# Seven-product MLP chunks: which engine makes which sum and low part, and in which order the loads come

## The reference, cut to what matters

```python
u = modulate(h, sh_f, sc_f)
y = jnp.square(jax.nn.relu(u @ mlp_w_up[layer])) @ mlp_w_down[layer]
h = layer_norm(DEEPNORM_ALPHA * h + (1 + g_f) * y, ...)
```

## Time and profile before

| | |
|---|---|
| median of 3 runs | 2198.15 us (2197.61 to 2199.14) |
| the profiled execution | 2198.61 us |
| its span, first to last instruction | 2196.9 us |
| TensorE's granted clock, mean | 0.997 of full speed |
| TensorE busy | 2144.9 us, 98% |
| VectorE, ScalarE, GpSimd busy | 1419.3, 820.0, 373.6 us |

### The profile page before, as it was taken

The page is one execution under the profiler, slowest core; times in us unless marked ns, Lnnn a source line. Parts: engine busy times, 40 slices in busy tenths (PEclk is TensorE's granted clock), DMA queues, the critical chain, the costliest instruction groups (busy, mean ns, idle before and its releaser), DMA issues.

```text
span 2196.9 us, 28310 instructions
## 1 busy us (share of the span) xinstructions
PE 2144.9 (98%) x9984; PEld 1730.2 (79%) x9984; DVE 1419.3 (65%) x2223; ACT 820.0 (37%) x1457; POOL 373.6 (17%) x273
## 2 busy tenths in 40 slices
PE   6999999999999999999999999999999999999998
PEld 5888888878887787788887876677888888888886
DVE  7423656578576676776768566767747547557556
ACT  4201445161224234233347456546222422422432
POOL 0000220010033032130200022321003303303304
PEclk9999999999999999999999999999999999999999
DMA  7434653314413423314122110211211021021021
GB/s 291 142 98 133 117 131 101 105 39 134 130 63 95 125 66 115 113 59 134 48 96 85 43 39 20 78 58 33 64 58 58 21 74 57 20 75 57 19 77 77
DMA packets 52433, 183.96 MB, mean 84 GB/s; under 512 B 7472, under 2 KB 7648, under 8 KB 52352
## 3 DMA queue, kind: packets, MB, share of 16 engines
q1 hardware_dynamic: 44640, 161.50, 22.8%
q0 software_dynamic: 4944, 16.96, 3.6%
q10 hardware_dynamic: 2768, 4.41, 0.5%
HBM read 174.43 MB, written 8.42 MB: 83 GB/s over the span
## 4 chain that ended last, share of the span: by engine, by line
issue 44%; PE 41%; POOL 8%; DVE 3%; ACT 2%; DMA 1%; SPq 1%; POOLq 0%; ACTq 0%; DVEq 0%
PE ps L2054 11%; PE ps L2056 11%; PE ps L2055 11%; POOL whi L678 4%; POOL wlo L678 2%; PE ps L2519 1%; POOL h_blocks L673 1%; PE ps L2549 1%; PE ps L2533 1%; DMA resid<-in_xt 1%; PE ps L2157 1%; PE ps L2298 1%; PE ps L2283 1%; PE ps L2287 1%; DVE stats L1572 0%
## 5 line engine op out<-in xcount | busy, mean ns | idle before, releaser
L2054 PE MATMUL ps<-uhi,whi 128*128 128x512 f32 x1152 | 451.6, 392 | 11.3 <-DVE wlo L1700 5.0
L2055 PE MATMUL ps<-ulo,whi 128*128 128x512 f32 x1152 | 448.4, 389 | 0.0
L2056 PE MATMUL ps<-uhi,wlo 128*128 128x512 f32 x1152 | 448.3, 389 | 0.0
L2054 PE MATMUL ps<-whi,uhi 128*128 128x512 f32 x704 | 288.2, 409 | 2.4 <-ACT resid L1111 2.2
L2056 PE MATMUL ps<-whi,ulo 128*128 128x512 f32 x704 | 276.1, 392 | 0.0
L2055 PE MATMUL ps<-wlo,uhi 128*128 128x512 f32 x704 | 275.4, 391 | 0.0
L2054 PEld LDWEIGHTS ps<-uhi,whi 128*128 128x128 f32 x1152 | 216.2, 188 | 65.2 <-issue 7.3
L1740 DVE TENSOR_TENSOR resid<-ps,resid 128x512 f32<-128x512 f32 x336 | 217.9, 680 | 54.8 <-PE ps L2056 53.7
L2056 PEld LDWEIGHTS ps<-uhi,wlo 128*128 128x128 f32 x1152 | 216.3, 188 | 45.3
L2055 PEld LDWEIGHTS ps<-ulo,whi 128*128 128x128 f32 x1152 | 216.3, 188 | 44.0
L1021 ACT ACTIVATE h_blocks<-ps 128x512 f32<-128x512 f32 x96 | 57.2, 596 | 516.5 <-PE ps L2056 516.5
(11 more groups left out here) (300 smaller groups left out, 3542.1 us busy)
## 6 DMA issues: line engine op xcount, KB each, us to landing
stage<-in_stream SPq DMA_DIRECT2D x276, 512.0 KB, 3.6
aux<-in_early SPq DMA_DIRECT2D x8, 512.0 KB, 7.1
early_place<-in_early SPq DMA_DIRECT2D x8, 512.0 KB, 14.2
resid<-in_xt SPq DMA_DIRECT2D x8, 512.0 KB, 15.9
resid<-in_x POOLq DMA_DIRECT2D x8, 512.0 KB, 9.5
resid_dram<-resid ACTq DMA_DIRECT2D x8, 512.0 KB, 2.6
resid<-resid_dram POOLq DMA_DIRECT2D x8, 512.0 KB, 3.6
out<-resid SPq DMA_DIRECT2D x7, 512.0 KB, 2.6
```

What stands on the lines that cost most here:

```text
L2054: pe.matmul(dst, left_hi, right_hi, start=start, stop=False, skip_group_check=more)
L2055: pe.matmul(dst, left_hi, right_lo, start=False, stop=False, skip_group_check=more)
L2056: return pe.matmul(dst, left_lo, right_hi, start=False, stop=stop, skip_group_check=more)
```

## The change

Four parts, all in the twelve chunks made of seven products; chunks 0 and 7 and the rest of the kernel stay as they are. The arithmetic is the same, the engines and the order differ.

- S2 (h7) and S4 (h8) are both made by VectorE in halves of 128x512 (`second_sum`, `fourth_sum`) among the half sums; GpSimd's S2 and its semaphore go.
- The low part of P2's weights (w_part 4, 2; B21) goes from GpSimd to VectorE, behind the low of h1.
- GpSimd's four other weight low parts each wait until VectorE has made the activation's low part of the same product (a new wait on `h_low` ahead of each). VectorE's order of adds and low parts changes; `up_low(8)` and `up_low(9)` move behind adds of P6.
- In the streamed chunks up-weight 2 comes after vector 1 and up-weight 3 after vector 2, so each stands one place earlier in the stream, and vector 3 comes among the last five.

```diff
@@ load_order @@
-            ada(SC_KV + c, range(3))
+            ada(SC_KV + c, range(2))
             w(W_MLP0 + 8 * c + 2)
-            ada(SC_KV + c, range(3, 4))
+            ada(SC_KV + c, range(2, 3))
             w(W_MLP0 + 8 * c + 3)
-            ada(SC_KV + c, range(4, K))
+            ada(SC_KV + c, range(3, K))
...
@@ GpSimd, seven_sums @@
-                pool.wait_ge(h_low, 8 * q0 + 3 + 8 * i)
-                pool.tensor_tensor(h_block(7), h_block(6), h_block(0), ALU.subtract).then_inc(h_sums_by_pool, 1)
-                def low_by_pool(n, hi, lo):
+                def low_by_pool(after, n, hi, lo):
+                    pool.wait_ge(h_low, 8 * q0 + after + 8 * i)
                     pool.wait_ge(operand_hi, 15 * q0 + n + 15 * i)
...
-                low_by_pool(7, 4, 2)
-                low_by_pool(9, 5, 0)
-                low_by_pool(11, 1, 7)
-                low_by_pool(13, 8, 6)
-                low_by_pool(15, 4, 3)
+                low_by_pool(5, 9, 5, 0)
+                low_by_pool(6, 11, 1, 7)
+                low_by_pool(7, 13, 8, 6)
+                low_by_pool(8, 15, 4, 3)
@@ VectorE, seven_chunk @@
+                def weight_low(hi, lo, n):
+                    v.wait_ge(operand_hi, 15 * q0 + n + 15 * i)
+                    v.tensor_tensor(w_part(lo), w_block(lo), fr(w_part(hi)), ALU.subtract).then_inc(w_low, 1)
...
+                def second_sum(f):
+                    v.wait_ge(h_sums, 7 * q0 + 2 + 3 * f + 7 * i)
+                    v.tensor_tensor(h_block(7)[:, f, :], h_block(6)[:, f, :], h_block(0)[:, f, :],
+                                    ALU.subtract).then_inc(h_sums, 1)
+                def fourth_sum(f):
+                    v.wait_ge(h_sums, 7 * q0 + 3 + 3 * f + 7 * i)
+                    v.tensor_tensor(h_block(8)[:, f, :], h_block(1)[:, f, :], h_block(7)[:, f, :],
+                                    ALU.subtract).then_inc(h_sums, 1)
...
                 if with_ada:
-                    for k in range(3):
+                    for k in range(2):
                         vector(k)
                 up_low(2)
                 if with_ada:
-                    vector(3)
+                    vector(2)
                 up_low(3)
...
-                    for k in range(4, K):
+                    for k in range(3, K):
                         vector(k)
                 half_sum(0)
                 half_low(0)
+                second_sum(0)
+                fourth_sum(0)
                 half_sum(1)
+                second_sum(1)
                 half_low(1)
-                add("P7", 0, 1, 2)
-                v.wait_ge(h_sums_by_pool, q0 + 1 + i)
-                v.tensor_tensor(h_block(8), h_block(1), h_block(7), ALU.subtract).then_inc(h_sums, 1)
-                add("P7", 3)
-                v.wait_ge(h_sums, 4 * q0 + 4 + 4 * i)
-                add("P4", 0)
+                fourth_sum(1)
+                add("P7", 0, 1, 2, 3)
+                v.wait_ge(h_sums, 7 * q0 + 7 + 7 * i)
                 low_of(4, 1, 6)
-                add("P4", 1, 2, 3)
+                weight_low(4, 2, 7)
+                add("P4", 0, 1)
                 low_of(5, 0, 8)
+                add("P4", 2, 3)
                 add("P2", 0, 1)
                 low_of(2, 7, 10)
                 add("P2", 2, 3)
                 add("P1", 0)
                 low_of(3, 6, 12)
-                add("P1", 1)
+                add("P1", 1, 2, 3)
+                low_of(4, 8, 14)
+                add("P6", 0, 1, 2)
                 up_low(8)
-                add("P1", 2, 3)
+                add("P6", 3)
                 up_low(9)
-                add("P6", 0)
-                low_of(4, 8, 14)
-                add("P6", 1, 2, 3)
                 add("P5", 0, 1, 2, 3)
```

More of the change, by code:

```diff
@@ L445, in build @@
         h_sums = sem("h_sums")
-        h_sums_by_pool = sem("h_sums_by_pool")
         h_low = sem("h_low")
@@ L1030, in seven_up @@
                         high(w_part(1), w_block(8))
-                        act.wait_ge(h_sums, 4 * q0 + 1 + 4 * i)
+                        act.wait_ge(h_sums, 7 * q0 + 1 + 7 * i)
                         high(h_part(4), h_block(5))
                     if u >= 6:
-                        act.wait_ge(h_sums, 4 * q0 + u - 4 + 4 * i)
+                        act.wait_ge(h_sums, 7 * q0 + 2 + 3 * (u - 6) + 7 * i)
                         high(h_part(2)[:, u - 6, :], h_block(3)[:, u - 6, :])
@@ L1043, in seven_up @@
                 done("P4")
-                act.wait_ge(h_sums_by_pool, q0 + 1 + i)
+                act.wait_ge(h_sums, 7 * q0 + 6 + 7 * i)
                 high(h_part(2), h_block(7))
@@ L1049, in seven_up @@
                 done("P2")
-                act.wait_ge(h_sums, 4 * q0 + 4 + 4 * i)
+                act.wait_ge(h_sums, 7 * q0 + 7 + 7 * i)
                 high(h_part(4), h_block(8))
@@ L1759, in seven_chunk @@
                 v.tensor_tensor(h_block(5), h_block(0), h_block(2), ALU.subtract).then_inc(h_sums, 1)
-                for n, hi, lo in ((1, 4, 5), (2, 1, 8)):
-                    v.wait_ge(operand_hi, 15 * q0 + n + 15 * i)
-                    v.tensor_tensor(w_part(lo), w_block(lo), fr(w_part(hi)), ALU.subtract).then_inc(w_low, 1)
+                weight_low(4, 5, 1)
+                weight_low(1, 8, 2)
                 low_of(4, 5, 3)
                 if with_ada:
-                    for k in range(4, K):
+                    for k in range(3, K):
                         vector(k)
@@ L2425, in down @@
                         last.then_inc(group_done, 1)
-                pe.wait_ge(w_low, 2 * q0 + 1 + 2 * i)
+                pe.wait_ge(w_low, 3 * q0 + 1 + 3 * i)
                 pe.wait_ge(h_low, 8 * q0 + 1 + 8 * i)
@@ L2431, in seven_chunk @@
                 down("P7", (4, 5), (4, 5), True)
-                pe.wait_ge(w_low, 2 * q0 + 2 + 2 * i)
+                pe.wait_ge(w_low, 3 * q0 + 2 + 3 * i)
                 pe.wait_ge(h_low, 8 * q0 + 3 + 8 * i)
                 down("P4", (2, 3), (1, 8), False, after="P7")
-                pe.wait_ge(w_low_by_pool, 5 * q0 + 1 + 5 * i)
+                pe.wait_ge(w_low, 3 * q0 + 3 + 3 * i)
                 pe.wait_ge(h_low, 8 * q0 + 4 + 8 * i)
                 down("P2", (4, 1), (4, 2), True, after="P4")
-                pe.wait_ge(w_low_by_pool, 5 * q0 + 2 + 5 * i)
+                pe.wait_ge(w_low_by_pool, 4 * q0 + 1 + 4 * i)
                 pe.wait_ge(h_low, 8 * q0 + 5 + 8 * i)
                 down("P1", (5, 0), (5, 0), True)
-                pe.wait_ge(w_low_by_pool, 5 * q0 + 3 + 5 * i)
+                pe.wait_ge(w_low_by_pool, 4 * q0 + 2 + 4 * i)
                 pe.wait_ge(h_low, 8 * q0 + 6 + 8 * i)
@@ L2445, in seven_chunk @@
                     sum_quarters(1 + i, NUMBER["ada", SC_KV + 1, K - 1] + 1 + per * i)
-                pe.wait_ge(w_low_by_pool, 5 * q0 + 4 + 5 * i)
+                pe.wait_ge(w_low_by_pool, 4 * q0 + 3 + 4 * i)
                 pe.wait_ge(h_low, 8 * q0 + 7 + 8 * i)
@@ L2450, in seven_chunk @@
                     turn_quarters(1 + i)
-                pe.wait_ge(w_low_by_pool, 5 * q0 + 5 + 5 * i)
+                pe.wait_ge(w_low_by_pool, 4 * q0 + 4 + 4 * i)
                 pe.wait_ge(h_low, 8 * q0 + 8 + 8 * i)
```

## The result

| | before | after |
|---|---|---|
| median of 6 runs each, same chips | 2199.16 us | 2178.64 us (2177.64 to 2179.47) |
| ratio, 95% interval | | 0.9907 (0.9894 to 0.9919) |
| the profiled execution, its span | 2198.61, 2196.9 us | 2177.64, 2175.9 us |
| VectorE, GpSimd busy | 1419.3, 373.6 us | 1395.6, 271.1 us |

What follows compares the result with a forecast made beforehand. TensorE, busy 98% of the span, was taken to bound the kernel, so only its waits could be given back. 9.6 + 6.8 + 3.4 - 2.1 = 17.7 us off the median of 2198.15 gave 2180.5 us, range 2177 to 2190.

Steps and rivals of the forecast that it cites:

- Loads: Streamed chunks, ahead of up-groups u=4 and u=5: both stops go with the earlier up-weights, 9.6 us gained.
- Ports: All twelve chunks: VectorE's low parts no longer stretched by GpSimd's, stops ahead of P2 (6.8 us) and inside P6 (3.4) go.
- S2 and S4 in a chunk without vectors: Layer 1's six chunks: the halves on VectorE cost nothing, with 0.8 us to spare before P4.
- S2 and S4 in a streamed chunk: Six streamed chunks: a new stop ahead of P4's first tile, 0.35 us each with restart, 2.1 us lost.
- The sum: Whole kernel: 17.7 us less than the median 2198.15, giving 2180.5 us, -0.8%; chance 0.72.
- P4's stop as a serious cost: Rival, streamed chunks: VectorE comes later, P4 waits 1.5 us each, 10.5 us lost, 2188.9 us; chance 0.12.
- Only the loads pay: Rival: stops ahead of P2 and inside P6 stay because B21's low part is late on VectorE, 2190.7 us; chance 0.07.
- Next to nothing: Rival: TensorE's stops come from the stream or itself and return at the same places, 2197 us; chance 0.05.
- The slower outcome: Rival, streamed chunks: vector 7 lands later, half_sum(0) slips and P4 stops, 25 us lost, 2203 us; chance 0.04.
- What the trace was to show: Signs: low parts 1.2 and 2.4 us, waits for lines 1716 and 1700 and P6's stop gone, short new P4 wait.

Runs made afterwards that it cites:

- e1: The kernel before with only the loads and VectorE's vectors in the changed order: 2187.92 us, ratio 0.9946.
- e2: The changed kernel with the loads and VectorE's vectors put back in the order of before: 2187.82 us, ratio 0.9943.
- e7: The changed kernel with up-weights 2 and 3 one place earlier still, behind vectors 0 and 1: 2189.78 us, ratio 0.9958.
- e8: The kernel before with GpSimd's new waits alone, on all five weight low parts: 2207.59 us, ratio 1.0042.
- e3: The changed kernel without GpSimd's new waits on VectorE's low parts: 2180.91 us, ratio 0.9914.
- e4: The changed kernel with B21's low part back on GpSimd, behind VectorE's low of h1: 2179.05 us, ratio 0.9909.
- e5: The changed kernel with S2 back on GpSimd and S4 whole on VectorE: 2178.82 us, ratio 0.9908.
- e9: The kernel before with the new loads and VectorE's changed order, but S2 and B21's low part on GpSimd, S4 whole, no new waits: 2197.72 us, ratio 0.9998.

## Why the prediction was right, step by step

- **Loads** (up-weights 2 and 3 one place earlier), 9.6 us: right, 9.93 alone (e1). Both up-weights came early enough; u = 4 and u = 5 start without a stop in all six chunks.
- **Ports** (the stops ahead of P2 and inside P6), 6.8 + 3.4 = 10.2 us: right in kind, 1 us short. Layer 1 gives 0.97 us a chunk and not 0.85, e2 11.2 in all. The two stops were summed from the two steps around each that stood out; the chunk's pitch holds all that they cost, and would have been the better row: the matmuls after a stop go on starting a few ns late each.
- **S2 and S4 in a chunk without vectors**, nothing: right, no stop in layer 1.
- **S2 and S4 in a streamed chunk**, 2.1 us lost: right place, too large. The two parts together fall 1.2 us short of their sum. Half_sum(0) started at 684.81, 1.65 us before ScalarE read the last up-group (686.46); worked out had been about 1.0 (688.2 against 689.2). And it was not chunk 1 that was spared, as I had thought: it waited longest, 0.26 us, and the others less or not at all.
- **The sum**: 17.7 against 20.5 in the medians. Of the 2.8 missing, 1.0 is the ports' term, 0.9 the stop ahead of P4, 0.3 the loads, and the rest lies in stretches that the change does not touch.
- **The rivals.** P4's stop as a serious cost was real but not here: e7 shows that one more vector ahead of half_sum(0) brings it to 1.7 us. "Only the loads pay" would have been about the time of e1, and the rest of the change gives 10 us more in the chunks. "Next to nothing" falls, since the stops are gone and came back nowhere. The slower outcome did not come. The way priced for it, vectors that come later, shows in e7 as the 12.2 us given back; e8, the waits alone, is 0.4% slower by a way that was not priced, P2 waiting for GpSimd's B21.
- **What the trace was to show** it showed: low parts at 1.22 and 2.4 us, no wait for line 1716 or 1700, no stop in P6. The pitch of layer 0's chunks fell by 14.13 / 6 = 2.36 us; the 2.3 to 2.8 given for it did not follow from the sum itself, whose terms make (9.6 + 5.1 - 2.1) / 6 = 2.1.
- **Two readings were off** and moved no term. P4 of chunk 1 began at 610.53, not 610.7. And 677.9, given for the low of h5 in the streamed chunk, is by that working the time when vector 3 is used: the low part, 2 us earlier than before, would be done at 676.7.

What carries the gain is that no part of GpSimd is under way when VectorE comes to the low of h1, and that VectorE comes to it early. Several forms do that (e3, e4, e5 each undo one of the means and lose 2.6, 0.5 and 0.3 us; in e4 B21's part is on GpSimd behind the low of h1 as in e8, but that low comes early, and P2 hardly stops). Taking one of the means without the other (the waits in e8, VectorE's order in e9) loses all of this part's gain. Which form is best by itself is not settled below a microsecond.

## What to carry to other kernels

When two engines take turns at a resource, count who starts first in front of the one operation that the bound engine waits for, and then what stands behind that operation in its queue: e9 moved P4's first add behind it, and two more behind the next such operation, and turned a wait of 0.3 us into two of 1.2 together. Order by an added wait only if the delayed part has room: waits ahead of all five parts cost 9 us in the old order, where P2 waits for the first of them (e8), and those ahead of the other four save 2.6 us in the new one (against e3). Where single parts are worth a microsecond, cut the traces at fixed points around the changed loop: there two profiles of one kernel agreed to 0.3 us, where whole times spread by 2.

## What the runs showed of the hardware

A VectorE subtraction of two SBUF tensors that comes up while GpSimd runs one waits until GpSimd's has ended. In e9 GpSimd starts at 1650.96 and takes 2.4 us, to 1653.36; VectorE's starts at 1651.08 and ends 1.1 us after that, 3.38 us in all for an operation of 1.22. The profile shows such a wait as a longer operation, not as idle time. Additions of a PSUM and an SBUF tensor were never held: of the 336 in the kernel before, the 168 that overlap one of GpSimd's operations take 677 ns on average and 684 at most, the others 684 and 693. The SBUF page of the Trainium skill (SBUF — State Buffer, "SBUF: two separate sides") says both: whichever of the two starts first has the shared port pair for its whole instruction, and outside the 2-port modes a VectorE operation contends for it only with two SBUF inputs. These rows agree. A stop costs more than its wait: P2's 0.31 us and P6's, which the view of waits leaves out, together made each of layer 1's chunks 0.97 us longer.
